# Three weight tiles multiplied row block by row block behind a norm, the last square of a norm added in PSUM, and an early Ln

## The chip, the cores and the metric

The kernel runs on one core of one Trainium2 chip. The metric is the device time of one execution in microseconds (us). A core has five engines that work at the same time, each through its own list of instructions, and wait for each other on semaphores: TensorE (PE; its weight loads are PEld), VectorE (DVE), ScalarE (ACT), GpSimd (POOL) and SyncE (SP), which issues most DMAs. SBUF is the memory that the engines work from; PSUM takes what TensorE multiplies and can add to what is there.

## The reference

Two transformer stacks follow each other on one sequence of 256 tokens with 1024 features. Everything is fp32. The first has two layers (one with attention, one with a gated delta rule), the second has two layers of `FFN, mixer with latent attention, FFN`, and also carries 256 context tokens. What matters here is what stands between them all the time, a norm with modulation and then a linear:

```python
def rmsnorm(x, g):
    xf = x.astype(jnp.float32)
    y = xf * lax.rsqrt(jnp.mean(xf * xf, axis=-1, keepdims=True) + EPS)
    return (y * g.astype(jnp.float32)).astype(x.dtype)

def ffn_half_step(s, m, i, norm_g, w_in, w_out):
    h = modulate(rmsnorm_2(s, norm_g), m, i)
    gu = h @ w_in
    y = (jax.nn.silu(gu[..., :D_FF]) * gu[..., D_FF:]) @ w_out
    return s + 0.5 * gate(m, i) * y
```

There are twelve norms: ten with modulation and a linear behind them, one between the two stacks, directly followed by a modulated one, and the final one. The modulation vectors come from products of one or two condition vectors with wide matrices.

## The kernel before

Activations lie with the features on the partitions: `x` is 8 blocks (`KD`) of 128 features by 256 or 512 columns (tokens; `T` is 256, and 512 are the tokens and the context). A linear is a row of weight tiles, each 1024 rows by 128 output features. The tiles of all linears are numbered through (`g`), and live in a ring of 4 slots (`RING`) in SBUF, with 4 PSUM banks for their results. To multiply in fp32r with enough precision, each number is split in a high and a low part: per 128 rows of a tile there are three products (`w_hi`*`h_hi`, `w_lo`*`h_hi`, `w_hi`*`h_lo`), 24 for a tile.

For one tile, SP loads `raw`; ScalarE casts it to `w_hi` (`split`, L1607), once TensorE is through with the tile 4 before; VectorE computes `w_lo` (L1716). TensorE multiplies (L1488). The result leaves PSUM through VectorE or ScalarE (`epilogue`). Each engine goes through the tiles in its own loop: ScalarE in step j first casts tile g+4 and then does the epilogue of tile g, VectorE first computes `w_lo` of tile g+3 (`AHEAD`), then, in some linears, the row sums of a hosted modulation unit, then the epilogue. A hosted unit is 8 scaled additions of weight rows (`ada_rows`, L1733, doubled for the two conditions of the second stack) in four portions, spread over tiles by `hosted_units`; TensorE turns the sum at a given tile (`unit_sums`, L1498) and waits there for the rows. The first unit's four portions are at tiles 0, 1, 2, 3 of the linear `ffn1_w_in_2` layer 0, with the sum behind tile 3; in `ffn2_w_in_2` layer 0 at 0, 1, 3, 4 (sum behind 4), in `ffn_w_in` layer 0 and `ffn1_w_in_2` layer 1 at 0, 2, 4, 6 (behind 6), in `attn_w_in` at 0, 2, 5, 8 (behind 8).

A norm starts in the residual linear ahead of it. As VectorE adds each of its 8 tiles to `x` (L1813), ScalarE squares the block (L1630) into one of two buffers `sq`, and VectorE adds it to `ssq` (L1833). When the eighth is added, TensorE sums over the partitions by a product with ones in fp32 (`norm_sums`, L1512), ScalarE takes Ln (L1677) and Exp (L1678) for the reciprocal root. Each function needs its table in ScalarE; the compiler puts an ACT_TABLE_LOAD before an instruction that needs another one. Then VectorE scales a block (L1924), ScalarE shifts and rounds it to `h_hi` (L1687), VectorE computes `h_lo` (L1916), block by block, with two streams of 256 columns where the norm has 512. TensorE begins tile 0 of the next linear with block 0 as soon as it is there, and waits for each block; tiles 1, 2 follow when tile 0 is done. `w_hi` and `w_lo` of tiles 0, 1, 2 are ready by then, except behind the first norm, where VectorE computes those of tiles 1 and 2 behind the norm's blocks.

Of the kernel before, what the change touches and what calls it, by code (L numbers as in the profile page):

```python
# [14 lines left out]
P = 128  # L15
D = 1024
KD = D // P
T = 256
# [14 lines left out]
AHEAD = 3  # L33
BODY = 4
# [205 lines left out]
def number(stages):  # L240

    g = h_blocks = a_blocks = norms = subs = silus = sqs = ssqs = 0
    slot_dmas = [0] * RING
    tiles = []
    conv = 0
    for i, s in enumerate(stages):
        if isinstance(s, Linear):
# [18 lines left out]
            if s.kind == "residual" and s.more["last"]:  # L266
                sqs += KD
                ssqs += 1
        elif s[0] == "setup":
            sqs += KD  # L270
            ssqs += 1
        elif s[0] == "norm":
            n = KD * s[3] // T
            stages[i] = ("norm", *s[1:], dict(n=norms, subs=subs, sq=sqs, ssq=ssqs, h=h_blocks))
            norms += 1
            if s[1] == "mod":
                h_blocks += n
                subs += n
            if s[1] == "replace":
                sqs += KD  # L280
                ssqs += 1
        elif s[0] == "attention":
            stages[i] = ("attention", h_blocks)
            h_blocks += KD
        elif s[0] == "delta":
            stages[i] = ("delta", h_blocks)
            h_blocks += HEADS
        elif s[0] == "mixer":
            own = 1 if s[1] else 2
            stages[i] = ("mixer", s[1], h_blocks)  # L290
            h_blocks += 4 * own
        elif s[0] == "mla":
            own = 1 if s[1] else 2
            stages[i] = ("mla", s[1], h_blocks)
            h_blocks += 4 * own
# [4 lines left out]
def build(nc, dram, out, stages):  # L300
# [4 lines left out]
    with ExitStack() as stack:  # L305
# [29 lines left out]
        tmp = sb("tmp", [P, 4, T])  # L335
        heads_c = sb("heads_c", [P, 2, HEADS])
# [1133 lines left out]
        def _(pe):  # L1470
            mm, tr = nc.tensor.matmul, nc.tensor.transpose

            def tile(lin, j, h_waits):
                g = lin.g0 + j
                slot = g % RING
                m = lin.columns(j)
                n = lin.tokens
# [3 lines left out]
                pe.wait_ge(s_lo, g + 1)  # L1481
                if g >= RING:
                    pe.wait_ge(s_evac, g - RING + 1)
                for k in range(lin.kt):
                    if h_waits is not None:
                        pe.wait_ge(*h_waits(k))
                    for w, v in ((w_hi, hi), (w_lo, hi), (w_hi, lo)):
                        last = mm(ps[0:m, slot, 0:n], w[:, slot, k * P:k * P + m], v[:, s0 + k, 0:n],  # L1488
                                  start=(k == 0 and w is w_hi and v is hi), stop=(k == lin.kt - 1 and v is lo))
                last.then_inc(s_tile, 1)  # L1490
# [18 lines left out]
            def norm_sums(tokens, ready):  # L1509

                pe.wait_ge(s_ssq, ready)
                mm(ps[:, NORM_BANK, 0:tokens], ones, ssq[:, 0:tokens], start=True, stop=True).then_inc(s_ssT, 1)  # L1512
# [16 lines left out]
            def linear(lin):  # L1529
                w = waits(lin)  # L1530
                for j in range(lin.n):
                    tile(lin, j, w if j == 0 else None)
                    if lin.g0 + j in sum_at:
                        unit_sums(sum_at[lin.g0 + j])

            for st in stages:
# [20 lines left out]
                elif st[0] == "modulation":  # L1557
                    for k in range(2, KD):
                        first_products(k)
                    norm_sums(T, 1)  # L1560
# [5 lines left out]
                elif st[0] == "norm":  # L1566
                    at_ = st[4]
                    if at_["n"]:
                        norm_sums(st[3], at_["ssq"])
# [28 lines left out]
        def _(act):  # L1598
# [10 lines left out]
            def epilogue(lin, j):  # L1609
# [18 lines left out]
                elif lin.kind == "residual" and lin.more["last"]:  # L1628
                    act.wait_ge(s_evac, g + 1)
# [79 lines left out]
        def _(dve):  # L1709
# [119 lines left out]
            def add_squares(k, n):  # L1829
# [4 lines left out]
                if k == KD - 1:  # L1834
# [26 lines left out]
            for st in stages:  # L1861
                if isinstance(st, Linear):
# [17 lines left out]
                    if squared:  # L1880
                        squares(st, KD - 1)
# [12 lines left out]
                elif st[0] == "norm":  # L1894
# [38 lines left out]
                    elif mode == "replace":  # L1933
                        g = vec_at["final_norm_g"]

                        def add(k):
# [5 lines left out]
                            if k == KD - 1:  # L1942
# [10 lines left out]
                        add(KD - 1)  # L1953
# [41 lines left out]
```

## Time and profile before

| what | value |
|---|---|
| time, median of 3 runs | 2861.45 us (2860.23 to 2862.41) |
| time of the profiled execution | 2862.04 us |
| its span, first to last instruction | 2860.2 us |
| mean granted TensorE clock, as a share of 2.4 GHz | 0.951 |
| TensorE busy | 2579.6 us, 90% |
| VectorE busy | 1791.7 us, 63% |
| ScalarE busy | 1038.6 us, 36% |
| GpSimd busy | 53.3 us, 2% |
| chain that ended last: PE, DVE, ACT | 82%, 9%, 5% |

Busy is the time in which an engine runs an instruction; what it waits for is in the list of waits. The chain that ended last is followed back from the last instruction, at each step to what released it. The granted clock is what the chip's throttle allowed TensorE; it knows two levels here, 1.0 (2.4 GHz) and 0.5 (1.2 GHz). Instructions overlap a little, so that the start of the next can lie before the end of the one ahead. 1.8 us lie outside the span.

### The profile page before, as it was taken

What the parts mean: (1) busy time and instruction counts of PE and PEld (TensorE: products, weight loads), DVE (VectorE), ACT (ScalarE), POOL (GpSimd) and SP (SyncE); (2) the same over time, 40 slices, a digit from 0 to 9 for tenths busy, and PEclk for the clock granted to TensorE, in tenths of its full rate; (3) what the DMA queues carried; (4) which work ended last, traced back from release to release, by engine and by line L of the source; (5) the groups of instructions that cost most, each with busy time, mean ns of one, the idle gap of its engine ahead of it and who ended that gap; (6) DMA issues with size and microseconds to landing.
All of it is one profiled execution on the core that took longest, in us unless ns stands there. A gap on an engine that the chain in (4) does not pass through costs nothing.

```text
span 2860.2 us, 37126 instructions
## 1 busy us (share of the span) xinstructions
PE 2579.6 (90%) x14954; PEld 2176.4 (76%) x14954; DVE 1791.7 (63%) x2952; ACT 1038.6 (36%) x1571; POOL 53.3 (2%) x56
## 2 busy tenths in 40 slices
PE   5888998876899889999897989999999999889998
PEld 4748998855799868888675568888778888766998
DVE  3647778644465677777745666666766565765655
ACT  4465435521254542222313442222332222434543
POOL 1000000020100000000000000000000000000000
PEclk9989999988999989999998999999999999899999
DMA  8776885522456646555312035555544444331563
GB/s 271 209 228 205 256 247 160 164 67 67 126 156 187 189 118 162 155 161 153 98 44 69 8 103 155 153 135 150 151 116 135 145 140 126 101 79 47 160 188 114
DMA packets 632561, 407.56 MB, mean 142 GB/s; under 512 B 27752, under 2 KB 588615, under 8 KB 631367
## 3 DMA queue, kind: packets, MB, share of 16 engines
q1 hardware_dynamic: 631712, 404.94, 49.1%
q8 instruction: 119, 1.95, 0.3%
q14 instruction: 52, 0.42, 0.0%
q10 hardware_dynamic: 678, 0.25, 0.0%
HBM read 404.09 MB, written 1.05 MB: 142 GB/s over the span
## 4 chain that ended last, share of the span: by engine, by line
PE 82%; DVE 9%; ACT 5%; DMA 2%; issue 1%; SPq 0%; ACTq 0%; POOL 0%; DVEq 0%
PE ps L1488 70%; DVE tmp L1924 1%; PE ps L1269 1%; PE ps L1498 1%; DVE h_lo L1916 1%; PE ps L1246 1%; DVE ada_acc L1733 1%; PE ps L789 1%; PE ps L526 1%; ACT w_hi L1607 1%; PE ps L797 1%; PE ps L799 1%; PE ps L1258 1%; ACT L1678 1%; DMA raw<-in_w_out 0%
## 5 line engine op out<-in xcount | busy, mean ns | idle before, releaser
L1488 PE MATMUL ps<-h_hi,w_hi 128*128 128x256 f32 (+1 forms) x3048 | 1018.5, 334 | 70.7 <-DVE h_lo L1916 60.1
L1607 ACT CAST w_hi<-raw 128x1024 fp32r<-128x1024 f32 (+3 forms) x557 | 555.0, 997 | 1383.1 <-PE ps L1488 1359.2
L1488 PE MATMUL ps<-h_hi,w_lo 128*128 128x256 f32 (+1 forms) x3048 | 1005.7, 330 | 0.0
L1488 PE MATMUL ps<-h_lo,w_hi 128*128 128x256 f32 (+1 forms) x3048 | 1005.4, 330 | 0.0
L1716 DVE TENSOR_TENSOR w_lo<-raw,w_hi 128x1024 fp32r<-128x1024 f32 (+3 forms) x557 | 645.0, 1158 | 351.8 <-ACT w_hi L1607 349.3
L1488 PEld LDWEIGHTS ps<-h_hi,w_hi 128*128 128x128 f32 x3048 | 587.1, 193 | 143.8 <-issue 68.1
L1488 PEld LDWEIGHTS ps<-h_lo,w_hi 128*128 128x128 f32 x3048 | 588.5, 193 | 50.2
L1488 PEld LDWEIGHTS ps<-h_hi,w_lo 128*128 128x128 f32 x3048 | 589.1, 193 | 47.0
L1488 PE MATMUL ps<-a_hi,w_hi 128*128 128x256 f32 (+1 forms) x1056 | 356.9, 338 | 0.1
L1488 PE MATMUL ps<-a_hi,w_lo 128*128 128x256 f32 (+1 forms) x1056 | 355.5, 337 | 0.0
L1488 PE MATMUL ps<-a_lo,w_hi 128*128 128x256 f32 (+1 forms) x1056 | 355.5, 337 | 0.0
L1733 DVE SCALAR_TENSOR_TENSOR ada_acc<-ada_raw,cond,ada_acc 128x512 f32<-128x512 f32 x490 | 349.0, 748 | 6.6 <-DMA ada_raw<-in_ada_w 0.9
L1488 PEld LDWEIGHTS ps<-a_hi,w_hi 128*128 128x128 f32 x1056 | 199.3, 189 | 24.6 <-DVE a_lo L1770 0.7
L1488 PEld LDWEIGHTS ps<-a_lo,w_hi 128*128 128x128 f32 x1056 | 199.2, 189 | 24.3
L1488 PEld LDWEIGHTS ps<-a_hi,w_lo 128*128 128x128 f32 x1056 | 199.2, 189 | 24.0
L1813 DVE SCALAR_TENSOR_TENSOR x<-ps,coef,x 128x256 f32<-128x256 f32 x256 | 116.3, 480 | 141.9 <-PE ps L1488 140.7
L1784 DVE TENSOR_TENSOR a_f<-silu_g,ps 128x256 f32<-128x256 f32 (+1 forms) x132 | 73.1, 554 | 147.5 <-PE ps L1488 96.2
L1770 DVE TENSOR_TENSOR a_lo<-a_f,a_hi 128x256 fp32r<-128x256 f32 (+1 forms) x132 | 72.9, 552 | 15.1 <-ACT a_hi L1618 15.1
L1924 DVE SCALAR_TENSOR_TENSOR tmp<-x,coef,rstd 128x256 f32<-128x256 f32 x120 | 55.6, 477 | 27.5 <-ACT rstd L1678 27.5
L1687 ACT ACTIVATE h_hi<-tmp,coef 128x256 fp32r<-128x256 f32 x120 | 58.8, 506 | 31.9 <-DVE tmp L1924 31.9
L1618 ACT CAST a_hi<-a_f 128x256 fp32r<-128x256 f32 (+1 forms) x132 | 67.1, 508 | 1.8 <-DVE a_f L1784 1.8
L1615 ACT ACTIVATE silu_g<-ps 128x256 f32<-128x256 f32 (+1 forms) x132 | 63.9, 484 | 0.1
(313 smaller groups left out, 1889.2 us busy)
## 6 DMA issues: line engine op xcount, KB each, us to landing
raw<-in_ffn_w_in SPq DMA_DIRECT2D x264, 512.0 KB, 4.5
ada_raw<-in_w_mod SPq DMA_DIRECT2D x120, 512.0 KB, 3.9
raw<-in_ffn_w_out SPq DMA_DIRECT2D x96, 512.0 KB, 4.5
ada_raw<-in_ada_w SPq DMA_DIRECT2D x40, 512.0 KB, 5.3
wide_rows<-in_ada_w SPq DMA_DIRECT2D x40, 512.0 KB, 4.8
raw<-in_ffn_w_out SPq DMA_DIRECT2D x48, 384.0 KB, 3.4
raw<-in_gdn_w_in SPq DMA_DIRECT2D x33, 512.0 KB, 4.1
raw<-in_w_in SPq DMA_DIRECT2D x26, 512.0 KB, 3.9
```

What stands on the lines that cost most here:

```text
L526: last = nc.tensor.matmul(ps[32 * j:32 * j + 32, bank, :].rearrange("p (a n) -> p a n", a=2), cond_wide[:, k, :], wide_rows[i % 2][:, 2 * ...
L1488: last = mm(ps[0:m, slot, 0:n], w[:, slot, k * P:k * P + m], v[:, s0 + k, 0:n], start=(k == 0 and w is w_hi and v is hi), stop=(k == lin.k ...
L1607: nc.scalar.copy(w_hi[:, slot, 0:n], raw[:, slot, 0:n]).then_inc(s_hi, 1)
L1615: A(silu_g[:, (j // 2) % 2, 0:n], ps[:, slot, 0:n], ACT.Silu).then_inc(s_silu, 1)
L1618: nc.scalar.copy(a_hi[:, j // 2, 0:n], a_f[:, (j // 2) % 2, 0:n]).then_inc(s_ahi, 1)
L1687: A(h_hi[:, k, cols(c)], tmp[:, i % 4], ACT.Identity, bias=coef[:, c, 1, k:k + 1]).then_inc(s_nhi, 1)
L1716: V.tensor_tensor(w_lo[:, slot, 0:n], raw[:, slot, 0:n], w_hi[:, slot, 0:n].bitcast(F32), ALU.subtract).then_inc(s_lo, 1)
L1733: last = V.scalar_tensor_tensor(out=ada_acc[:, c], in0=rows[:, i], scalar=cond[:, col:col + 1], in1=ada_acc[:, c], op0=ALU.mult, op1=ALU.add)
L1770: V.tensor_tensor(a_lo[:, pair, 0:n], a_f[:, pair % 2, 0:n], a_hi[:, pair, 0:n].bitcast(F32), ALU.subtract).then_inc(s_alo, 1)
L1784: V.tensor_tensor(a_f[:, pair % 2, 0:n], silu_g[:, pair % 2, 0:n], bank, ALU.mult).then_inc(s_evac, 2)
L1813: last = V.scalar_tensor_tensor(out=x[:, j, cols(c)], in0=ps[:, slot, cols(c)], scalar=coef[:, c, 2, j:j + 1], in1=x[:, j, cols(c)], op0=A ...
L1924: V.scalar_tensor_tensor(out=tmp[:, (i0 + m) % 4], in0=x[:, k, cols(c)], scalar=coef[:, c, 0, k:k + 1], in1=rstd[:, cols(c)], op0=ALU.mult ...
```

## The change

Three edits.

- In a linear that directly follows a norm, TensorE takes the first three tiles (`TOGETHER`) together: for each of the 8 row blocks it waits for the block of `h`, then does the three products of tile 0, of tile 1 and of tile 2, into three banks. All three end with the last block. Any unit sum that is due at one of them comes behind all three. Other tiles are done as before.
- The eighth square of a norm is no longer added to `ssq` by VectorE. `ssq` is signalled with seven blocks in it, and TensorE does a second product with ones over the eighth block in `sq`, into the same bank (over the columns that are new, `fresh`; the context's sums stay in `ssq` through the norm between the stacks). The first norm keeps its sum.
- In the last tile of the residual linear that ends in a norm, ScalarE runs Ln on one column of a constant (`table_seed`), behind the cast of tile g+4 and ahead of its wait for the tile and of the square. It is there for ten of the twelve norms: not for the first, and not for the one behind the norm between the stacks.

```diff
--- before.py
+++ after.py
@@ -31,6 +31,7 @@
 MOD1, MOD2 = 6, 9
 RING = 4
 AHEAD = 3
+TOGETHER = 3
 BODY = 4
 X_BANKS = (1, 2, 3, 6)
 FIRST_UNITS = 4
@@ -241,6 +242,7 @@
 
     g = h_blocks = a_blocks = norms = subs = silus = sqs = ssqs = 0
     slot_dmas = [0] * RING
+    fresh = T
     tiles = []
     conv = 0
     for i, s in enumerate(stages):
@@ -264,6 +266,7 @@
                 silus += s.n
                 conv += s.n * 3 if s.kind == "delta_in" else 0
             if s.kind == "residual" and s.more["last"]:
+                fresh = s.tokens
                 sqs += KD
                 ssqs += 1
         elif s[0] == "setup":
@@ -271,12 +274,13 @@
             ssqs += 1
         elif s[0] == "norm":
             n = KD * s[3] // T
-            stages[i] = ("norm", *s[1:], dict(n=norms, subs=subs, sq=sqs, ssq=ssqs, h=h_blocks))
+            stages[i] = ("norm", *s[1:], dict(n=norms, subs=subs, sq=sqs, ssq=ssqs, h=h_blocks, fresh=fresh))
             norms += 1
             if s[1] == "mod":
                 h_blocks += n
                 subs += n
             if s[1] == "replace":
+                fresh = s[3]
                 sqs += KD
                 ssqs += 1
         elif s[0] == "attention":
@@ -333,6 +337,7 @@
         sq = sb("sq", [P, 2, 2 * T])
         rstd = sb("rstd", [P, 2 * T])
         tmp = sb("tmp", [P, 4, T])
+        table_seed = sb("table_seed", [P, 1])
         heads_c = sb("heads_c", [P, 2, HEADS])
         base = nc.sbuf_base
         limit = nc.sbuf_usable_end
@@ -1470,24 +1475,28 @@
         def _(pe):
             mm, tr = nc.tensor.matmul, nc.tensor.transpose
 
-            def tile(lin, j, h_waits):
-                g = lin.g0 + j
-                slot = g % RING
-                m = lin.columns(j)
-                n = lin.tokens
+            def tiles_together(lin, js, h_waits):
+
                 src = lin.more.get("source", "h")
                 s0 = lin.more.get("source0", 0)
                 hi, lo = {"h": (h_hi, h_lo), "a": (a_hi, a_lo), "lat": (lat_hi, lat_lo)}[src]
-                pe.wait_ge(s_lo, g + 1)
-                if g >= RING:
-                    pe.wait_ge(s_evac, g - RING + 1)
+                n = lin.tokens
                 for k in range(lin.kt):
                     if h_waits is not None:
                         pe.wait_ge(*h_waits(k))
-                    for w, v in ((w_hi, hi), (w_lo, hi), (w_hi, lo)):
-                        last = mm(ps[0:m, slot, 0:n], w[:, slot, k * P:k * P + m], v[:, s0 + k, 0:n],
-                                  start=(k == 0 and w is w_hi and v is hi), stop=(k == lin.kt - 1 and v is lo))
-                last.then_inc(s_tile, 1)
+                    for j in js:
+                        g = lin.g0 + j
+                        slot = g % RING
+                        m = lin.columns(j)
+                        if k == 0:
+                            pe.wait_ge(s_lo, g + 1)
+                            if g >= RING:
+                                pe.wait_ge(s_evac, g - RING + 1)
+                        for w, v in ((w_hi, hi), (w_lo, hi), (w_hi, lo)):
+                            last = mm(ps[0:m, slot, 0:n], w[:, slot, k * P:k * P + m], v[:, s0 + k, 0:n],
+                                      start=(k == 0 and w is w_hi and v is hi), stop=(k == lin.kt - 1 and v is lo))
+                        if k == lin.kt - 1:
+                            last.then_inc(s_tile, 1)
 
             def unit_sums(unit):
 
@@ -1506,10 +1515,15 @@
                               start=(k == 0), stop=(k == KD - 1))
                 last.then_inc(event("first_rows_multiplied"), 1)
 
-            def norm_sums(tokens, ready):
-
-                pe.wait_ge(s_ssq, ready)
-                mm(ps[:, NORM_BANK, 0:tokens], ones, ssq[:, 0:tokens], start=True, stop=True).then_inc(s_ssT, 1)
+            def norm_sums(tokens, at_):
+
+                pe.wait_ge(s_ssq, at_["ssq"])
+                one = at_["n"] == 0
+                last = mm(ps[:, NORM_BANK, 0:tokens], ones, ssq[:, 0:tokens], start=True, stop=one)
+                if not one:
+                    pe.wait_ge(s_sq, at_["sq"])
+                    last = mm(ps[:, NORM_BANK, 0:at_["fresh"]], ones, sq[:, (KD - 1) % 2, 0:at_["fresh"]], start=False, stop=True)
+                last.then_inc(s_ssT, 1)
 
             def waits(lin):
 
@@ -1528,8 +1542,12 @@
 
             def linear(lin):
                 w = waits(lin)
+                i = next(n for n, s in enumerate(stages) if s is lin)
+                together = TOGETHER if not isinstance(stages[i - 1], Linear) and stages[i - 1][0] == "norm" else 1
+                tiles_together(lin, range(together), w)
                 for j in range(lin.n):
-                    tile(lin, j, w if j == 0 else None)
+                    if j >= together:
+                        tiles_together(lin, [j], None)
                     if lin.g0 + j in sum_at:
                         unit_sums(sum_at[lin.g0 + j])
 
@@ -1557,7 +1575,7 @@
                 elif st[0] == "modulation":
                     for k in range(2, KD):
                         first_products(k)
-                    norm_sums(T, 1)
+                    norm_sums(T, dict(n=0, ssq=1))
                     pe.wait_ge(s_vec, 2)
                     pe.wait_ge(event("first_sums_copied"), 1)
                     for q in range(4):
@@ -1566,7 +1584,7 @@
                 elif st[0] == "norm":
                     at_ = st[4]
                     if at_["n"]:
-                        norm_sums(st[3], at_["ssq"])
+                        norm_sums(st[3], at_)
                     if st[1] == "final":
                         for k in range(KD):
                             pe.wait_ge(s_nt, at_["subs"] + k + 1)
@@ -1626,6 +1644,8 @@
                     f = ACT.Silu if t0 < 32 else ACT.Copy
                     A(dst, y_conv[:, j % 2], f).then_inc(s_silu, 1)
                 elif lin.kind == "residual" and lin.more["last"]:
+                    if j == lin.n - 1:
+                        A(table_seed[:], const("eps"), ACT.Ln)
                     act.wait_ge(s_evac, g + 1)
                     A(sq[:, j % 2, 0:n], x[:, j, 0:n], ACT.Square).then_inc(s_sq, 1)
 
@@ -1831,7 +1851,7 @@
                     last = V.tensor_copy(ssq[:, 0:n], sq[:, 0, 0:n])
                 else:
                     last = V.tensor_tensor(ssq[:, 0:n], ssq[:, 0:n], sq[:, k % 2, 0:n], ALU.add)
-                if k == KD - 1:
+                if k == KD - 2:
                     last.then_inc(s_ssq, 1)
                 else:
                     link(dve, last, "dve")
@@ -1877,8 +1897,6 @@
                         epilogue(st, j)
                         if squared and j:
                             squares(st, j - 1)
-                    if squared:
-                        squares(st, KD - 1)
                 elif st[0] == "setup":
                     V.memset(cond_wide[:], 0.0)
                     V.memset(vec_in[:], 0.0).then_inc(s_zero, 1)
@@ -1939,7 +1957,7 @@
                                 last = V.tensor_copy(ssq[:, 0:T], sq[:, 0, 0:T])
                             else:
                                 last = V.tensor_tensor(ssq[:, 0:T], ssq[:, 0:T], sq[:, k % 2, 0:T], ALU.add)
-                            if k == KD - 1:
+                            if k == KD - 2:
                                 last.then_inc(s_ssq, 1)
                             else:
                                 last.then_inc(event("middle_added"), 1)
@@ -1950,7 +1968,6 @@
                                                    op0=ALU.mult, op1=ALU.mult).then_inc(event("middle_normed"), 1)
                             if k:
                                 add(k - 1)
-                        add(KD - 1)
                     else:
                         g = vec_at["final_norm_2"]
                         for k in range(KD):
```

## Rows read from the trace of the kernel before

**Rows 1.** the page's first part: busy us (share) and instructions of the engines

```profile
PE 2579.6 (90%) x14954; PEld 2176.4 (76%) x14954; DVE 1791.7 (63%) x2952; ACT 1038.6 (36%) x1571; POOL 53.3 (2%) x56
```

**Rows 2.** list of waits, TensorE: line, waited for, us in total, times, longest

```profile
PE ps L1488 <- DVE h_lo L1916: 60.1, 27, 6.5
PE ps L1498 <- DVE ada_acc L1733: 19.1, 13, 3.0
```

**Rows 3.** timeline, ScalarE, norm at 2649: start, us, instruction, [idle before <-releaser]

```profile
2646.98 1.04 ACT L1607 CAST w_hi<-raw 128x1024 fp32r<-128x1024 f32 x1 [1.51 <-PE ps L1488]
2647.93 0.41 ACT L1630 ACTIVATE sq<-x 128x256 f32<-128x256 f32 x1
2648.36 1.28 ACT L1677 ACT_TABLE_LOAD   x1
2649.66 0.47 ACT L1677 ACTIVATE rstd<-ps,consts 128x256 f32<-128x256 f32 x1
```

**Rows 4.** timeline, TensorE, the same norm

```profile
2648.92 0.70 PE L1512 MATMUL ps<-ssq,consts 128*128 128x256 f32 x2 [2.04 <-DVE ssq L1833]
```

**Rows 5.** timeline, norm of 512 columns at 2073, ScalarE and TensorE

```profile
2070.18 1.04 ACT L1607 CAST w_hi<-raw 128x1024 fp32r<-128x1024 f32 x1 [2.62 <-PE ps L1488]
2072.60 1.13 PE L1512 MATMUL ps<-ssq,consts 128*128 128x512 f32 x2 [2.52 <-DVE ssq L1833]
2073.77 0.69 ACT L1677 ACTIVATE rstd<-ps,consts 128x512 f32<-128x512 f32 x1 [0.71 <-PE ps L1512]
```

**Rows 6.** instructions of L881 and L885: duration ns min/median/max, first and last start

```profile
L881 ACT ACTIVATE gates<-gates x1: 216/216/216, 562.9 to 562.9; 128x16 f32<-128x16 f32 x1
L885 ACT ACTIVATE sq<-proj x8: 613/620/627, 563.0 to 573.3; 128x512 f32<-128x512 f32 x8
```

**Rows 7.** timeline, ScalarE, final norm

```profile
2843.93 0.42 ACT L1630 ACTIVATE sq<-x 128x256 f32<-128x256 f32 x1 [1.62 <-DVE x L1813]
```

**Rows 8.** L1488 by windows: us, PE busy (x), PEld busy (x), PEclk, DMA, GB/s

```profile
457.35:469.30 11.95, 11.95 (x73) 11.62 (x74) 0.74 0.24 65
1011.78:1033.90 22.12, 20.33 (x74) 14.34 (x75) 0.89 0.34 94
2465.09:2482.60 17.51, 14.13 (x74) 12.29 (x75) 0.65 0.23 61
```

**Rows 9.** the same view, two stretches at full clock, 256 and 512 columns

```profile
500.00:520.00 20.00, 20.00 (x169) 20.00 (x168) 1.00 0.64 175
2110.00:2130.00 20.00, 19.36 (x86) 15.73 (x85) 1.00 0.56 158
```

**Rows 10.** timeline, TensorE, two blocks behind the norm at 2459

```profile
2466.57 0.58 PE L1488 MATMUL ps<-h_hi,w_hi 128*128 128x256 f32 x1 [0.51 <-DVE h_lo L1916]
2468.16 0.58 PE L1488 MATMUL ps<-h_hi,w_hi 128*128 128x256 f32 x1 [0.57 <-DVE h_lo L1916]
```

**Rows 11.** timeline, VectorE, `delta_in`

```profile
465.50 1.22 DVE L1716 TENSOR_TENSOR w_lo<-raw,w_hi 128x1024 fp32r<-128x1024 f32 x1
468.58 1.21 DVE L1716 TENSOR_TENSOR w_lo<-raw,w_hi 128x1024 fp32r<-128x1024 f32 x1
```

**Rows 12.** timeline, VectorE and TensorE, behind the norm at 1006

```profile
1026.36 2.86 DVE L1733 SCALAR_TENSOR_TENSOR ada_acc<-ada_raw,cond,ada_acc 128x512 f32<-128x512 f32 x4
1039.11 1.04 PE L1498 MATMUL ps<-consts,ada_acc 128*128 128x128 f32 x8
```

**Rows 13.** timeline, TensorE, first unit sum behind the norm at 239

```profile
267.63 0.66 PE L1498 MATMUL ps<-consts,ada_acc 128*128 128x128 f32 x4 [1.02 <-DVE ada_acc L1733]
```

**Rows 14.** timeline, VectorE and TensorE, behind the first norm

```profile
51.93 3.48 DVE L1716 TENSOR_TENSOR w_lo<-raw,w_hi 128x1024 fp32r<-128x1024 f32 x3
79.50 0.66 PE L1498 MATMUL ps<-consts,ada_acc 128*128 128x128 f32 x4 [3.02 <-DVE ada_acc L1733]
```

**Rows 15.** instructions of L1677 and L1678: table loads

```profile
L1677 ACT ACT_TABLE_LOAD  x12: 1283/1283/1283, 39.9 to 2844.4; - x12
L1678 ACT ACT_TABLE_LOAD  x12: 1283/1283/1283, 41.7 to 2846.2; - x12
```

## The prediction

> **What bounds the kernel now.** I read the page first. TensorE is busy for nine tenths of the span [rows 1], and the chain of work that ended last runs through it for 82%. So time comes from the gaps between its products, or from its clock. The list of who TensorE waited for says where the gaps are [rows 2]: 60.1 us for VectorE's `h_lo` in front of the first products behind the norms, and 19.1 us at the transposes that end a hosted modulation unit. Then the timeline around two norms, one of 256 columns and one of 512. I name a norm by the time of its Ln.
>
> In the 256 column norm at 2649.66, ScalarE casts a weight tile when the last product is done, squares block 7, loads a table for Ln and runs Ln [rows 3]; a load for Exp follows. Beside that VectorE adds block 7 to `ssq`, and TensorE sums over the partitions from 2648.92, taking 0.70 [rows 4], until 2649.62. The load for Ln ends at 2648.36+1.28 = 2649.64. Sum and load end together: the load is hidden already. In the 512 column norm the sum ends about 0.7 us after the load [rows 5].
>
> **Part 1, the Ln seed.** The seed stands in ScalarE's program behind the cast for tile g+4, and that cast waits for the last tile of the linear, so it starts when TensorE has stopped [rows 3]. Loads run as soon as the instruction ahead is done: the one for Ln starts at 2648.36 although its data comes at 2649.62. So the seed's load would start at 2648.03, behind the cast and ahead of Square 7: 2648.03+1.29 = 2649.32, seed 0.22 (the row of a 128x16 ACTIVATE, the nearest [rows 6]; 0.15 to 0.28), Square from 2649.5 to 2649.9. The load leaves the cover of the adding and the summing and stands in front of both.
>
> **Part 2, the last square in PSUM.** The add of block 7 goes, a second fp32 product of the sum's size comes. The product over `ssq` now runs while ScalarE is still loading. The product over `sq` starts at 2649.96, takes 0.70, and Ln starts at 2650.70 with its table there. That is +1.04 against 2649.66. Square doesn't bring a load of its own: in the delta stage Square follows an Ln with no load between them [rows 6]. Five norms are of this form (239, 453, 797, 994, 2649): +5.2.
> For 512 columns: the cast ends at 2071.22, load and seed to 2072.73, Square 0.62 to 2073.34, product 1.13 to 2074.53, Ln at 2074.57 against 2073.77 [rows 5]: +0.8, four times (1398, 1685, 2073, 2459): +3.2. If the product meets the half clock that follows an idle TensorE, 0.4 to 0.85 more in some norms (range only).
> In the final norm no tile is left to cast, so the seed runs in ScalarE's idle 1.62 us before Square 7 [rows 7]: Ln about 0.2 earlier. The norm behind the middle one has no seed: one add less, one 256 column product more at the half clock, about +0.2. Sum of parts 1 and 2: **+8.4 us**, bounds 0 (load hidden) and +13 (half clock each time).
> The Trainium skill (ScalarE: Activation LUTs, What ACT_TABLE_LOAD costs) gives 1.283 us for the load and 1.38 more for a drain; the rows show the load and 0.02 behind it, so I don't add the drain. With it, the nine would cost 12 us more.
>
> **Part 3, three tiles behind a norm.** From the first product behind the norm to the end of the third tile, before: 72 products [rows 8]. At full clock a 256 column product takes 20/169 = 0.12 us and a 512 column one 0.233 [rows 9], so 72 would be 8.6 and 16.8 us, where 11.95 and 22.1 are spent. But the granted clock of these stretches is 0.74 and 0.89: the half level (1.2 GHz), behind an idle TensorE, for 2x0.26x11.95 = 6.2 us of the one and 4.9 of the other, from the front. There 0.213 a product is no less than the norm can feed with one 256 column tile: blocks come 0.79 apart (half of the 1.58 of two streams [rows 10]), three products take 0.64. So there is little idle to fill with 256 columns, more with 512 (blocks 1.58 apart [rows 10], three products 1.28 at half clock, 0.70 at full). With the half clock lasting as before:
> - 256 columns: about 6/0.213 = 28 products, 44 at 0.12: 11.3 for 11.95. A gain of 0.6 to 1.1.
> - 512 columns: 4.8/0.427 = 11, 61 at 0.233: 19.0 for 22.1. A gain of 3.1, taken as 2.8 at 2073, where the half clock held longer.
> - 256 column tiles behind the 512 column norm at 2459: the mean clock is 0.65 over 17.5 us, since one tile fills only 0.64 of each 1.58. Three tiles fill it, the clock returns during the norm, and the third tile ends 1.1 behind the last block: 11.5 for 17.5, a gain of 6.0.
>
> What comes next is VectorE and ScalarE. Before, their work on tile 0 (evacuation, the cast and `w_lo` of tile 4, and everything queued behind the wait for it) started when tile 0 ended. Now tile 0 ends six products before the third, so it starts 2 tiles less the gain later: some 4.5 us (256) and 7 us (512). TensorE has only tile 3 in hand. By norm:
> - 797, 2649: cast 1.05, `w_lo` 1.22, Silu's load and the evacuation reach tile 4's slot 2.6 us behind the trio's end, and tile 3 takes 2.88. Hidden by 0.3. Gain 1.0+1.1.
> - 1398, 2073, 2459: mixer or half as dense hosting. Tile 3 hides it. Gain 3.1+2.8+6.0.
> - 453 (`delta_in`): VectorE needs 3.08 us a tile against TensorE's 24x0.12 = 2.88 [rows 11], and lived on its lead: `w_lo` of tile 26 came 1.0 us ahead of its use. It now starts 4.5 later: 4.5-1.0 = +3.5; with a possibly earlier clock +3.2.
> - 1006 (`ffn1_w_in_2` 0, 512 columns): units are hosted in tiles 0, 1, 2, 3 and the sums are due behind tile 3. VectorE was busy without a break until those at 1039.11 [rows 12]. Now from the end of tile 0, S+17.5 (S = 1011.8, its first product): cast 1.1, w_lo 1.14, rows 2.77, a_f 0.6, w_lo 1.14, rows 2.77, a_lo 0.6, w_lo 1.14, rows 2.77 = 14.0, so 1043.3; transposes to 1044.5 against 1040.1: +4.4 (the trio's own gain is in it). TensorE is idle for 7 us before, as before a norm, so it resumes at the half clock. A microsecond at it costs 1-0.233/0.427 = 0.45; for 3.4 us (less than the 4.9 seen, since it is filled) +1.6. Together +6.0.
> - 1685 (tiles 0, 1, 3, 4; sums behind tile 4): the same sum gives the rows ready 15 us behind the trio's end, where TensorE is there after 11.2: +3.8 less the gain 3.2, and some half clock: +1.3.
> - 239 (256 columns, tiles 0, 2, 4, 6): rows ready 14.95 behind the trio's end against 11.5 for tile 6. It waited 1.0 before [rows 13]: 3.4-1.0-0.7 = +1.7.
> - the first norm: `w_lo` of tiles 1 and 2 stand behind the norm in VectorE's queue, in the three from 51.93 on [rows 14]. Tile 0 ran in that time, TensorE waiting 0.5 for tile 1. Now the trio stands from 47.6 to 54.2. Its end moves from 59.0 to 63.5, at 79.50, where a wait of 3.0 for the rows absorbs part [rows 14], +3 remain. SP's queue is also moved: the load of tile 8 waits for `w_lo` of tile 4, 7 us later. Bounds +1.5 and +6.
> Sum: gains -14.0, costs 3.2+6.0+1.3+1.7+3 = +15.2.
>
> **Total.** 8.4-14.0+15.2 = +9.6 on the profiled 2862.04, which is 0.6 above the median. From an earlier return of the clock in the filled stretches I take off 1.0: 2861.45+8.6 = **2870 us**.
>
> **Rivals.**
> (a) Not slower: VectorE's backlog hides. All trios then give their gain (4 norms of 256 about 4, 4 of 512 12, one 6: 22), only the first norm costs 3, the seeds 8.4: 2851. It decides at the first unit sum behind 1006: no wait there over 2 us. For it: VectorE is busy 63%. Against: it had no pause in that stretch [rows 12]. 0.12.
> (b) The clock comes back a step sooner because TensorE is never starved, and doesn't fall at the two stalls: 0.4 to 1.4 us in each of eight norms, 1.5 at 1006. 2864. 0.22, within 0.2%.
> (c) The seed costs nothing, the load being issued during the cast's wait: 2862. 0.05. Rows 3 speak against it, since loads start right behind the instruction ahead of them.
> (d) Ln and Exp share a load. If the seed's table served both, the load of 1.28 between Ln and Exp [rows 15], exposed in each of 11 norms, would go: -13, 2857. 0.03. The Trainium skill (ScalarE: Activation LUTs, Table sets) lists one set that holds both and counts one load for ln then exp; the trace disagrees, with 12 loads ahead of Ln and 12 ahead of Exp [rows 15].
> (e) Backlogs that last over several tiles, SP's loads late: over 2881. 0.10.
>
> **How the numbers follow.** Forecast (2867 to 2881) 0.48, (a) 0.12, (b) 0.22, (c) 0.05, (d) 0.03, (e) 0.10. Within 0.2% (5.7 us, about what can be told from no change) are (b), (c) and nothing of the forecast: 0.27. Faster: (a), (d): 0.15. Slower 0.58. The range leaves out (a), (d) and most of (e): 2859 to 2882; the forecast's own is 2867 to 2881.
>
> **What would show it.** An ACT_TABLE_LOAD between the cast and Square 7, none right before Ln; Ln 1.0 (256) and 0.8 (512) later behind the last product; TensorE idle about 7 us ahead of the transposes of the first unit behind 1006, and pauses of 0.2 a tile in `delta_in`; trio stretches of 11, 19 and 11.5 us. Wrong if the load costs nothing, or if VectorE keeps up.

## The result and the profile after

The changed kernel takes 2872.16 us (2870.59 to 2874.5, 6 runs) against 2861.12 before (2859.02 to 2862.41, 6 runs). The ratio is 1.0039, with an interval of 1.0027 to 1.005: slower by 11 us. The forecast was 2870 us, slower by 8.6.

The page of the changed kernel, its first part:

```profile
span 2868.5 us, 37158 instructions
PE 2585.0 (90%) x14976; PEld 2193.8 (76%) x14976; DVE 1783.3 (62%) x2941; ACT 1038.4 (36%) x1581; POOL 53.3 (2%) x56
```

Its list of what TensorE waited for (line, waited for, us in total, times, longest):

```profile
PE ps L1496 <- DVE h_lo L1934: 49.4, 12, 6.1
PE ps L1507 <- DVE ada_acc L1753: 30.7, 15, 7.5
...
PE ps L1525 <- ACT sq L1650: 9.3, 9, 1.7
```

The mean granted clock is 0.951 in both. Against [rows 2], the waits for `h_lo` come 12 times and not 27: within a norm TensorE is no longer starved. They fell by 10.7 us. The waits for a hosted unit's rows rose by 11.6. The wait of the new product for the last square is the third line, which has no counterpart before.

A 256 column norm of the changed kernel, to be laid beside [rows 3, 4]. The last product starts at 2651.38. The timeline of ScalarE:

```profile
2651.75 1.04 ACT L1625 CAST w_hi<-raw 128x1024 fp32r<-128x1024 f32 x1 [1.51 <-PE ps L1496]
2652.81 1.28 ACT L1648 ACT_TABLE_LOAD   x1
2654.10 0.20 ACT L1648 ACTIVATE table_seed<-consts 128x1 f32<-128x1 f32 x1
2654.21 0.40 ACT L1650 ACTIVATE sq<-x 128x256 f32<-128x256 f32 x1
2655.40 0.47 ACT L1697 ACTIVATE rstd<-ps,consts 128x256 f32<-128x256 f32 x1 [0.79 <-PE ps L1525]
2655.89 1.28 ACT L1698 ACT_TABLE_LOAD   x1
```

And of TensorE, with the two products with ones:

```profile
2652.57 0.70 PE L1522 MATMUL ps<-ssq,consts 128*128 128x256 f32 x2 [0.91 <-DVE ssq L1853]
2654.66 0.70 PE L1525 MATMUL ps<-sq,consts 128*128 128x256 f32 x2 [1.40 <-ACT sq L1650]
```

The load stands between the cast and the last square; the square starts 1.5 us later behind the last product than before. Ln starts 4.02 us behind the last product, 3.05 before. The load for Exp is there as it was.

A 512 column norm (the one at 2073 before), the timeline of ScalarE and TensorE from the square on:

```profile
2085.80 0.61 ACT L1650 ACTIVATE sq<-x 128x512 f32<-128x512 f32 x1
...
2086.47 2.08 PE L1525 MATMUL ps<-sq,consts 128*128 128x512 f32 x2 [0.53 <-ACT sq L1650]
...
2088.58 0.69 ACT L1697 ACTIVATE rstd<-ps,consts 128x512 f32<-128x512 f32 x1 [2.17 <-PE ps L1525]
```

Here the new product runs at the half clock: 2.08 us where the sum took 1.13 before [rows 5]. TensorE has done only one short product since the linear ended, 3.6 us before. That distance alone doesn't decide: at the norm at 1398 the new product also comes 3.6 us behind the last one and takes 1.13, at full clock.

The products of the linears by windows, in four trios (the three tiles taken together, from the first product behind the norm to the 72nd) and in two stretches of `delta_in`. Columns as in [rows 8]; the lines that answer to those are the second, third and fourth:

```profile
248.81:259.70 10.89, 10.89 (x74) 10.89 (x75) 0.79 0.31 96
467.11:478.10 10.99, 10.99 (x74) 10.99 (x75) 0.78 0.17 48
1029.43:1048.70 19.27, 19.27 (x73) 15.72 (x74) 0.85 0.20 55
2475.00:2486.90 11.90, 11.31 (x74) 10.71 (x75) 0.84 0.00 0
510.00:530.00 20.00, 20.00 (x158) 18.97 (x156) 1.00 0.68 180
530.00:550.00 20.00, 20.00 (x157) 19.10 (x158) 1.00 0.64 164
```

The trios took 11.0, 19.3 and 11.9 us where 72 products took 11.95, 22.1 and 17.5. In `delta_in` 158 products fit in 20 us at full clock, where 169 did [rows 9]: 24x20/158 = 3.04 us a tile, near VectorE's 3.08 [rows 11].

VectorE behind the norm of the first hosted unit (Ln at 1006 before), from the end of tile 0 on, and the transposes that wait for it:

```profile
1048.49 1.22 DVE L1736 TENSOR_TENSOR w_lo<-raw,w_hi 128x1024 fp32r<-128x1024 f32 x1 [5.44 <-ACT w_hi L1625]
1049.64 2.86 DVE L1753 SCALAR_TENSOR_TENSOR ada_acc<-ada_raw,cond,ada_acc 128x512 f32<-128x512 f32 x4
1052.42 0.68 DVE L1804 TENSOR_TENSOR a_f<-silu_g,ps 128x512 f32<-128x512 f32 x1
1053.01 1.22 DVE L1736 TENSOR_TENSOR w_lo<-raw,w_hi 128x1024 fp32r<-128x1024 f32 x1
1054.15 2.85 DVE L1753 SCALAR_TENSOR_TENSOR ada_acc<-ada_raw,cond,ada_acc 128x512 f32<-128x512 f32 x4
1056.92 0.68 DVE L1790 TENSOR_TENSOR a_lo<-a_f,a_hi 128x512 fp32r<-128x512 f32 x1
1057.53 1.22 DVE L1736 TENSOR_TENSOR w_lo<-raw,w_hi 128x1024 fp32r<-128x1024 f32 x1
1058.66 2.86 DVE L1753 SCALAR_TENSOR_TENSOR ada_acc<-ada_raw,cond,ada_acc 128x512 f32<-128x512 f32 x4
...
1061.57 0.69 PE L1507 MATMUL ps<-consts,ada_acc 128*128 128x128 f32 x2 [7.46 <-DVE ada_acc L1753]
```

VectorE waits 5.44 us for the cast of tile 4, that is for the end of tile 0, and then has thirteen microseconds of work queued. TensorE waits 7.46 for it.

**Where the time went.** I named the norms above by the time of their Ln in the kernel before, and do so here. I laid the two timelines side by side and took, at each norm, the difference of the two kernels at the last product ahead of it and at the first behind it. The change between these two is what the norm cost; the change from there until the casts run in step again is what the three tiles cost. Each column of times is from one execution. In us, beside the terms of the prediction:

| term | predicted | from the traces |
|---|---|---|
| Ln seed and product in PSUM, five norms of 256 columns | +5.2 | +6.6 (1.4, 0.9, 1.7, 1.7, 0.9) |
| the same, four norms of 512 | +3.2 | +4.8 (0.6, 1.6, 1.6, 1.1) |
| behind the middle norm; final norm | +0.2, -0.2 | +0.1, -0.2 |
| three tiles, first norm | +3 | +3.2 |
| at 239 | +1.7 | +2.9 |
| at 453 (`delta_in`) | +3.2 | +3.5 |
| at 1006 | +6.0 | +6.8 |
| at 1685 | +1.3 | +2.7 |
| at 797, 2649 | -1.0, -1.1 | -1.0, -0.6 |
| at 1398, 2073, 2459 | -3.1, -2.8, -6.0 | -4.0, -2.6, -5.3 |
| sum | +9.6 | +16.9 |

The last products of all lie 8.5 us apart, so some 8 us came back elsewhere, 4.2 of them between the norms at 1398 and 1685 (mixer and attention of the second stack) and 1.6 in the delta stage, without an edit there. The trace of the kernel with one tile behind a norm (below) gets back 3.2 us between 1398 and 1685 too, so most of it doesn't come from the three tiles; what it does come from is open. And within the residual linears, which the change doesn't touch, the kernels drifted: apart by half a microsecond every three tiles at 256 columns, together as fast at 512. That was in no part of the prediction. The mean distance between the starts of consecutive products at full clock (their pitch, in us), from all of them, tells why:

| kernel | a, 256 columns | a, 512 | h, 256 | h, 512 |
|---|---|---|---|---|
| before | 0.1135 | 0.2334 | 0.1200 | 0.2270 |
| changed | 0.1200 | 0.2269 | 0.1199 | 0.2269 |

(a: products that read `a_hi` or `a_lo`, some 1550 pairs each; h: 5100 and 3600 pairs.) The products of the residual linears had got slower at 256 columns and faster at 512.

### The profile page after: what moved, and what is told of

It is laid out like the page before. It is cut to its first block, busy times and chain, and to the rows that moved or that the text cites. A ratio compares the mean times of both kernels' runs of the same rounds, so it can differ in the third digit from the quotient of the medians.

```text
span 2868.5 us, 37158 instructions
## 1 busy us (share of the span) xinstructions
PE 2585.0 (90%) x14976; PEld 2193.8 (76%) x14976; DVE 1783.3 (62%) x2941; ACT 1038.4 (36%) x1581; POOL 53.3 (2%) x56
## 4 chain that ended last, share of the span: by engine, by line
PE 82%; DVE 8%; ACT 6%; DMA 2%; issue 2%; ACTq 0%; POOL 0%; SPq 0%; DVEq 0%
PE ps L1496 70%; DVE ada_acc L1753 2%; PE ps L1507 1%; PE ps L1274 1%; ACT w_hi L1625 1%; PE ps L1251 1%; PE ps L531 1%; PE ps L794 1%; PE ps L802 1%; DVE w_lo L1736 1%; PE ps L804 1%; DVE tmp L1942 1%; PE ps L1263 1%; ACT L1698 1%; PE ps L1235 0%
## 5 line engine op out<-in xcount | busy, mean ns | idle before, releaser
L1507 PE MATMUL ps<-consts,ada_acc 128*128 128x128 f32 x280 | 40.4, 287 | 30.7 <-DVE ada_acc L1753 30.7
```

What stands on the lines that cost most here:

```text
L1507: last = tr(ps[:, ADA_A + c, q * P:(q + 1) * P], ada_acc[:, c, q * P:(q + 1) * P], ident)
```

## The experiments

My theory in short: the load in front of the square costs 11 us, VectorE's late start costs more than the three tiles gain. And, new with the trace: the 4 bytes of `table_seed` moved `a_hi`, and that set the pitches.

The kernel before was measured again beside each kernel here, at 2861.85, 2862.82, 2861.98 or 2862.72 us, and every ratio is against that. Two kernels that weren't measured together can differ by 1 to 2 us for that reason alone, and the intervals are some 3 us to each side. So where a difference to the changed kernel matters, I give it also from the two distances to the kernel before (the changed kernel's is 11.0 us).

**Only the address.** The kernel before with one column more.

```diff
         tmp = sb("tmp", [P, 4, T])
+        unused = sb("unused", [P, 1])
```

> The kernel before with one unused 4 byte column between tmp and heads_c, and nothing else. It moves everything behind it, a_hi and a_lo by 64 bytes, as the changed kernel's table_seed does. Theory: where a_hi begins sets the pitch of the products that read it, so 256 column products go from 0.1135 to 0.120 us apart and 512 column ones from 0.233 to 0.227, some 1580 of each: +10 and -10, in all within 3 us of before, with the +10 partly hidden behind hosted units. Rival: the pitches changed with the order of TensorE's instructions, so this kernel keeps those of before and its time.

Measured 2861.39 us, ratio 0.9995 (0.9986 to 1.0005). The pitches of a are 0.1200 and 0.2268, those of h as before. So the drift is the address's, no instruction has part in it, and it nets to nothing here: it did not make the change slower.

**One tile behind a norm.**

```diff
-TOGETHER = 3
+TOGETHER = 1
```

> The changed kernel with one tile behind a norm (TOGETHER = 1). Theory (late VectorE): the three tiles cost more than they gain, 5 us in sum, so this is 2865 to 2868, with the 7 us wait behind the norm at 1006 gone. Rival (the seed costs more and the trios gain): over 2873.

Measured 2867.99, ratio 1.002 (1.0009 to 1.0031): 4.2 us under the changed kernel, 4.9 by the distances to the kernel before. The three tiles cost, in sum. TensorE's waits for a unit's rows are back at 18.7 us, none over 2.8. What is left, 6 us over before, is the seed with the product in PSUM; the traces of the norms had 11.3 for the two.

**No seed.**

```diff
-                    if j == lin.n - 1:
-                        A(table_seed[:], const("eps"), ACT.Ln)
```

> The changed kernel without the Ln on one column; its tile stays, so that addresses do. Theory: the load exposed ahead of the last square costs about 11 us over ten norms (dLn of 1.0 to 1.7), so 2860 to 2863, and Ln starts no later behind the last product than in the kernel before. Rival: the second product in PSUM makes the sum late, so Ln stays 0.5 or more late and the time falls by less than 5 us.

Measured 2862.88, ratio 1.0006 (0.9996 to 1.0015), 9.3 us under the changed kernel (10.0 by the distances to the kernel before). The timeline of its 256 column norm, ScalarE and TensorE:

```profile
2645.23 0.70 PE L1522 MATMUL ps<-ssq,consts 128*128 128x256 f32 x2 [0.91 <-DVE ssq L1851]
2645.37 0.41 ACT L1648 ACTIVATE sq<-x 128x256 f32<-128x256 f32 x1
2645.80 1.28 ACT L1695 ACT_TABLE_LOAD   x1
...
2645.83 0.70 PE L1525 MATMUL ps<-sq,consts 128*128 128x256 f32 x2
...
2647.09 0.47 ACT L1695 ACTIVATE rstd<-ps,consts 128x256 f32<-128x256 f32 x1
```

The sum is there at 2646.53, the load ends at 2647.08. The product in PSUM makes the sum half a microsecond earlier, and the load, back in its place, takes that away: Ln at 3.05 behind the last product, as before. At the 512 column norms it is at 3.98, for 4.07 before. At 256 columns the earlier sum is worth something only with an earlier load.

**The seed ahead of the cast**, where ScalarE waits for the last tile anyway.

```diff
-                    if j == lin.n - 1:
-                        A(table_seed[:], const("eps"), ACT.Ln)
...
+                        if st.kind == "residual" and st.more["last"] and j == st.n - 1:
+                            A(table_seed[:], const("eps"), ACT.Ln)
                         nxt = tile_of(st.g0 + j + AHEAD + 1)
                         if nxt:
```

> The changed kernel with the same Ln, but issued ahead of the cast of tile g+4 in the last tile, where ScalarE waits for TensorE 1.5 us (256 columns) or 2.6 us. Theory: the load is hidden there, and Ln can start when the sum is there, about 0.5 us earlier than before at 256 columns and the same at 512: 2 to 4 us under the kernel without the seed, 2857 to 2861. Rival: the load isn't what delays Ln, and this gives 2870 as the changed one.

Measured 2860.44, ratio 0.9992 (0.9983 to 1.0001), 11.7 us under the changed kernel (12.4 by the distances to the kernel before). Its 256 column norm, with the last product at 2639.30:

```profile
2638.18 1.28 ACT L1654 ACT_TABLE_LOAD   x1
2639.48 0.20 ACT L1654 ACTIVATE table_seed<-consts 128x1 f32<-128x1 f32 x1
2639.67 1.04 ACT L1625 CAST w_hi<-raw 128x1024 fp32r<-128x1024 f32 x1
2640.62 0.41 ACT L1648 ACTIVATE sq<-x 128x256 f32<-128x256 f32 x1
2641.82 0.47 ACT L1697 ACTIVATE rstd<-ps,consts 128x256 f32<-128x256 f32 x1 [0.79 <-PE ps L1525]
```

The same load runs under the last tile, and Ln starts 2.52 behind the last product, here and at 239 and 797. At the norms at 453 and 994 it starts at 3.14: there ScalarE has only 0.7 us free ahead of the cast, the load pushes the cast and the square by 0.6, and nothing is won. At the four norms of 512 columns it starts at 3.98, as without the seed. So the seed in its new place costs next to nothing and wins half a microsecond at three norms and 0.2 at the final one. That the kernel is faster than the one without the seed isn't shown (2860.4 and 2862.9, with intervals that overlap).

**One tile at the first hosted unit alone.** TensorE's wait there is to go, everything else stays.

```diff
-                together = TOGETHER if not isinstance(stages[i - 1], Linear) and stages[i - 1][0] == "norm" else 1
+                together = TOGETHER if not isinstance(stages[i - 1], Linear) and stages[i - 1][0] == "norm" and lin.weight != ("ffn1_w_in_2", 0) else 1
```

> The changed kernel, but with one tile behind the norm at 1006 (the linear ffn1_w_in_2 of layer 0), three behind the others. Theory (late VectorE): the 7.5 us wait for the first hosted unit's rows goes, and with it the 6.8 us that this linear's start lost: 2864 to 2867. Rival: the three tiles gain there as elsewhere, and the delay comes later or from the norm, so the time stays within 2 us of 2872.

Measured 2865.25, ratio 1.0007 (0.9997 to 1.0017), 6.9 us under the changed kernel where 6.8 were expected. That the two agree so closely is chance: by the distances to the kernel before (2.4 and 11.0) the difference is 8.6, and the intervals leave 4 us to each side. That this linear's start cost several microseconds is shown. In its list of waits of TensorE those for a unit's rows are back from 30.7 to 23.4:

```profile
PE ps L1507 <- DVE ada_acc L1753: 23.4, 14, 3.8
```

**Three tiles only where VectorE keeps up**, with the seed ahead of the cast: behind the norms at 797, 1398, 2073, 2459 and 2649.

```diff
-                together = TOGETHER if not isinstance(stages[i - 1], Linear) and stages[i - 1][0] == "norm" else 1
+                together = TOGETHER if not isinstance(stages[i - 1], Linear) and stages[i - 1][0] == "norm" and lin.weight not in (("attn_w_in", 0), ("ffn_w_in", 0), ("gdn_w_in", 0), ("ffn1_w_in_2", 0), ("ffn2_w_in_2", 0)) else 1
```

> Three tiles only behind the norms at 797, 1398, 2073, 2459 and 2649, the seed ahead of the cast, the square in PSUM. From the seed-ahead kernel (2860.4) the five linears with late VectorE give back what the trace shows for them: 3.2 (first norm) + 2.9 (239) + 3.5 (453) + 6.8 (1006) + 2.7 (1685) = 19, so 2839 to 2845. Rival: what is won at one norm is lost before the next stage, so 2852 or more.

Measured 2845.6, ratio 0.9941 (0.9927 to 0.9956), from 4 runs: just outside the expected range, 17 us under before, and 14.8 under the seed-ahead kernel (15.8 by the distances to the kernel before) where 19 were worked out. The direction and most of the size hold, and the rival of 2852 or more doesn't; the 3 to 4 us that are missing are no more than the noise.

**The address put to use.** These are kernels before, without the change's edits, in which a small switch (`Placed`) gives `a`, or `a` and `h`, one of two placements 64 bytes apart, by whether the stage has 256 or 512 columns. First I took the remainder of the address modulo 128 for the rule, for a alone and for both. For a alone, without the lines of the switch itself:

```diff
+        a_hi = Placed(a_hi, at("a_hi_64", 1 / 16, [P, KD, 2 * T], F32R), "a")
+        a_lo = Placed(a_lo, at("a_lo_64", 16 + 1 / 16, [P, KD, 2 * T], F32R), "a")
...
-        base = nc.sbuf_base
+        base = (nc.sbuf_base + 127) // 128 * 128
```

> The kernel before, with a_hi and a_lo read at two placements: 64 bytes past a multiple of 128 in linears of 256 columns, at the multiple in those of 512. Placement theory: 256 column products keep 0.1135, 512 column ones come to 0.227, 1580 times 0.0065: 10 us less, 2850 to 2853. Rival: the pitch isn't set by the address but by what surrounds a_hi, so one of the two pitches stays slow and the time is that of before.

> As the one above, and h_hi and h_lo too: in stages of 256 columns 64 bytes past a multiple of 128 (before: at the multiple in all). Placement theory: about 5370 products of 256 columns come from 0.120 to 0.1135 us apart, 35 us at most, less where VectorE sets the pace (delta_in, the linears with hosted units of the first stack): 12 to 28 us under the one above, 2823 to 2840. Rival (only a is sensitive): same time as above.

Measured 2860.03 (ratio 0.9996, 0.9986 to 1.0005) and 2870.83 (1.0039, 1.0023 to 1.0055). Both miss. The pitches of a were 0.1172 and 0.2268 in the one, 6 us lost at 256 columns for 10 won; in the other a had 0.1167 and 0.2326, h 0.1177 and 0.2325. So h is as sensitive as a, but modulo 128 is not the rule: 512 column data at a multiple of 128 had gone slow. The next try put each at exactly the remainders modulo 512 that had been fast in the kernel before (64 for 256 columns, 128 for 512). Its main lines, for h and for where a begins:

```diff
+        sb("pad_front", [P, 112])
...
+        sb("pad_back", [P, 16])
+        assert h_place % 512 == 64
+        h_hi = Placed(nc.alloc_sbuf_tensor_at("h_hi_64", [P, KD, 2 * T], F32R, offset=h_place + 64), h_hi, "h")
...
-        base = nc.sbuf_base
+        base = (nc.sbuf_base - 64 + 511) // 512 * 512 + 64
```

> The kernel before with both h and a read at two placements again, but now modulo 512: 64 past a multiple in stages of 256 columns (where a was before, pitch 0.1135), 128 past in those of 512 (where h was before, 0.227). The last kernel had 256 column data at 192 and 320 modulo 512 (0.1177 and 0.1167) and 512 column data at a multiple of 256 (0.2325). Theory (the residue modulo 512 decides, not 128): all 256 column products at 0.1135, all 512 ones at 0.227, so 10 us less for a at 512 columns and 15 to 30 for h at 256: 2822 to 2838. Rival (the distance to the weights' or another address decides): pitches between, and 2845 or more.

> The same placement with the chosen norms of three tiles, the seed ahead of the cast and the square in PSUM. If both hold they add up: the chosen kernel's 2845.6 less what the placement gives, 2808 to 2822; with the rival of the placement 2830 to 2846.

Measured 2833.49 (ratio 0.9914, 0.9891 to 0.9936) and, with the chosen norms, the seed ahead of the cast and the square in PSUM, **2811.39 us** (0.9831, 0.9813 to 0.9848): some 50 us under before, the best here (4 runs each). Products by windows in `delta_in` of the placed kernel without the change's edits, to be laid beside the 169 of [rows 9]:

```profile
480.00:500.00 20.00, 20.00 (x179) 20.00 (x178) 1.00 0.64 167
500.00:520.00 20.00, 19.62 (x160) 18.45 (x159) 1.00 0.64 176
```

In the first stretch TensorE runs at its new pitch; in the second fewer products fit in than before, 3.0 us a tile, near VectorE's 3.08 [rows 11]: it has used up VectorE's lead. So in `delta_in` little is won; the gain comes from the linears in which VectorE isn't the limit. The pitches were 0.1153 (h) and 0.1147 (a) at 256 columns and 0.2269 at 512; not quite 0.1135. Both times lie in the ranges of the theory, but the pitches lie between, as its rival said: the remainder modulo 512 isn't the rule, and the times were hit by a theory that doesn't hold.

**Own address or distance to the weights.** Twice the kernel before with 64 unused bytes, once in front of everything, once behind the weights.

```diff
+        unused = sb("unused", [P, 16])
         raw = sb("raw", [P, RING, SLOT])
```

> The kernel before with an unused tile of 64 bytes in front of raw, so that the weights (raw, w_hi, w_lo), h and a all lie 64 bytes further, at the same distances. If the distance to the weights sets the pitch, all pitches stay: a 0.1135 and 0.233, h 0.120 and 0.227. If the address of h and a themselves decides (h now at 192, a at 128 modulo 512), a goes to 0.120 and 0.227 as in the changed kernel, and h at 256 columns to 0.1177, as where it lay at 192 before.

```diff
+        unused = sb("unused", [P, 16])
         x = sb("x", [P, KD, 2 * T])
```

> The same 64 bytes behind the weights instead, in front of x: h and a move, the weights don't. Own address: the same pitches as the kernel with everything moved. Distance: pitches differ from that one, and a goes to 0.120 and 0.227.

| kernel | a, 256 | a, 512 | h, 256 | h, 512 | us (one run) |
|---|---|---|---|---|---|
| everything moved | 0.1134 | 0.2334 | 0.1200 | 0.2270 | 2860.14 |
| h and a moved, weights not | 0.1200 | 0.2271 | 0.1176 | 0.2290 | 2854.93 |

A stretch of `delta_in` at full clock by windows, with everything moved:

```profile
500.00:520.00 20.00, 20.00 (x169) 20.00 (x168) 1.00 0.61 163
```

And with h and a moved alone:

```profile
500.00:520.00 20.00, 20.00 (x172) 20.00 (x172) 1.00 0.66 179
```

Moving all leaves every pitch where it was, within 0.1 ns; moving the data against the weights changes all four. So what counts is the distance in SBUF between what a product streams and the buffers of the weights (`raw`, `w_hi`, `w_lo`), not an address. Those buffers are also written by DMAs, ScalarE and VectorE while TensorE multiplies, but that isn't what the pitch hangs on: of the pairs of products over `a` at 256 columns, 12 before and 13 in the changed kernel fell where no DMA packet and none of the other engines was active, and their pitches are 0.1133 and 0.1200, like those of all. That it is TensorE's own reading of the weights that meets its reading of the data is the explanation that is left, and not tested by itself. Which distances are good, in a formula, is open: the weights lie in four slots and two parts, and only a handful of placements was measured.

## Why the prediction was right

The time was 2.2 us above the forecast, inside its range and its own case. The steps, one by one:

- **The seed's place.** Right as drawn: cast, load, seed, square; no load at Ln; Ln 0.97 us late at full clock, for 1.04. For seed and product in PSUM together the sum had 8.4; the kernel with both and one tile behind a norm is 6 us over before, and removing the seed alone from the changed kernel gave 9.3 to 10.0 back. With intervals of 3 us these bear the term out, no more exactly than that. Rival (c), a seed that costs nothing, falls by the first rows above.
- **The half clock at the new product** was in the range and not in the sum. It happened at five of nine norms and for part of a sixth, which is the gap between 8.4 and 11.3 in the table. The term that was mis-sized is the 0.70 and 1.13 for the product: 1.2 and 2.1 us at the half clock. Where it happens isn't fixed: 3.3 us behind the last product it was at half at 239 and at full at 453, and at 2073, where it was at half here, it was at full at the same distance in the kernel with one tile. In the trace of the kernel with the unused column alone, the clock fell under the old sum at five norms, and Ln was up to 0.5 late there. So a part of these 2.9 us may be this execution's.
- **VectorE's late start**: right in kind at each of the five places, and 0.2 to 1.4 us too small at each. At 1006 the wait was 7.46 for a predicted 7, and taking that one linear out gave 6.9 us (8.6 by the distances to the kernel before). Rival (a), no wait over 2 us, falls there. Together with the gains the prediction had the three tiles at +1.2 us; by the traces they are at +5.6, and by the kernel with one tile at 4 to 5. That is the largest term that was too small.
- **The gains** were sized well: 11.0, 19.3 and 11.9 us for 11.3, 19.0 and 11.5. The gain is small at 256 columns and large at 512, as the reading said that TensorE at the half clock already used 0.64 of each 0.79 us. Rival (b), an earlier clock, seems to have come in part, since the half clock lasted 2x0.22x11 = 4.8 us at 453, for 6.2 before. But in the kernel with one tile it lasted 4.2 there, and the 72 products took 11.1: neither the shorter half clock nor most of the gain at 453 is shown to be the three tiles' doing. At 1006 and 2459 that kernel took 22.2 and 19.0, so the gains there are.
- **Shared tables** (rival (d)): the load ahead of Exp is there at every norm. Backlogs that go on growing (rival (e), over 2881) didn't come.
- **What I didn't see** is the address, that is, the placement of `a`. It moved 3100 products by 6.5 ns each, 10 us one way and 10 us the other. With only one of the two kinds of tiles, it would have been as large as the whole change. That the sum came out near is in part luck: these two cancelled, and the terms measured at the norms add up to 16.9 us, not 9.6, of which some 8 came back outside the norms. No run shows why they did.

## What to carry to other kernels

Before moving a table load "early", look what its engine's program waits for just ahead of the new place: a load that was hidden under another engine's work can land on the path, and one line higher it costs next to nothing where the engine waits there for longer than the load takes. When an engine is fed more at once, ask who starts late by that: here VectorE's queue was tied to the end of the first tile, and three tiles together paid only where its next work had slack. And when an edit adds a buffer, even of 4 bytes, compare the pitch of untouched inner loops in both traces before explaining the difference by the edit.

## What the runs showed of the hardware

The pitch of fp32r products depends on the distance in SBUF between the streamed operand and the weights' buffers. At full clock a 256 column product took 0.1135, 0.1167 to 0.1177, or 0.1200 us, a 512 column one 0.227, 0.229 or 0.233, at placements that lay multiples of 64 bytes apart; and the distances that were good for 256 columns were not those for 512. In this kernel that was worth some 25 us (ratio 0.9914, 0.9891 to 0.9936), more than any other edit here.

An ACT_TABLE_LOAD took 1.28 us each time in every row above, and didn't wait for what its own instruction waited for: in the kernel without the seed it began at 2645.80, 0.02 us behind the square, while the sum that Ln needs was there at 2646.53.
